# Reordering the attention stretch of a hybrid decoder step: three merged job streams, half-row gathers for every sample query, and prompt heads in pairs

## The chip, the cores and the metric

The program runs on one core of one Trainium2 chip. Its engines are TensorE (PE in the rows, with PEld for its weight loads), VectorE (DVE), ScalarE (ACT), GpSimd (POOL) and SyncE (SP). The metric is the device time of one execution, in microseconds. Runs of one kernel agree within about 0.3% as a rule.

## The reference, cut to what matters

One layer of a decoder is computed for a prompt of 512 tokens and for 64 sample tokens (8 sequences of 8), in f32. The part that this change touches is token mixing:

```python
def select_keys(scores, q_pos, topk):
    masked = jnp.where(key_pos <= q_pos, scores, -jnp.inf)
    _, idx = lax.top_k(masked, topk)

def attend_selected(q, kg, vg, valid):
    logits = jnp.einsum('bqhd,bqkhd->bqhk', q, kg) * (HEAD_DIM ** -0.5)
    p = jax.nn.softmax(jnp.where(valid, logits, -jnp.inf))
    return jnp.einsum('bqhk,bqkhd->bqhd', p, vg)

glu = a_glu * jax.nn.sigmoid(b_glu)
c = jax.nn.silu(layer_norm(causal_depthwise_conv(buf, conv_w, conv_b)))
conv_branch = c @ w_conv_out
attn_branch = o.reshape(B, T, ATT_W) @ w_attn_out
mix = (gc * conv_branch + ga * attn_branch) @ w_o
```

The prompt (8 heads of 64, 512 rows) attends to the 128 best keys of each row, the samples each to the 256 best keys out of 4096 cached ones and their own 8. For the samples the chosen rows of the cache are fetched: one row holds the key and the value of all heads, 2 x 512 f32. A mixture of experts follows, which the change does not touch.

## The kernel before

Every engine runs a list of instructions in a fixed order and waits on semaphores. The order of the stretch in question is computed in Python before the program is built, by a small model of the engines, and written out as two lists: ATTENTION (jobs of TensorE, which ScalarE follows in the same order) and VJOBS (VectorE's). The jobs:

- **Sample**, in 16 groups g of 4 queries. GpSimd issues the gathers (two indirect DMAs of 128 rows for each query). `T g.j` turns the keys of query j (8 transposes, `turn_keys`, L1116), `QK` computes logits (L1128, L1134), `EX` is the exponential on ScalarE, `PT` turns the weights (L1143, L1144), `PV` multiplies by the values (L1152, L1155), `OS` collects the rows (L1162). VectorE adds `max`, `sum` and `om` for each group. A group's gathers may start only when QK (for keys) and PV (for values, or whole rows) of the group before are done, since there is one set of buffers.
- **Prompt**. `pi t.h` gives the indexer's scores of tile t and head h (L1213). VectorE weighs and adds them (`pi`, L1942) and picks 128 keys of a row in 16 `round`s of MAX8 and MATCH_REPLACE8 (L1951, L1952); `bias` makes the mask. Then come 32 units u, 8 heads for each of 4 tiles, with 1 to 4 blocks of 128 keys: `qk u` (L1222), `unit u` on VectorE (L1958 to L1960), an exponential on ScalarE, `weigh u` on VectorE (L1967, L1968), `pt u` (L1229) and `pv u` (L1235). Tile 0 needs no mask from the rounds.
- **Branches**. Gates `gc` and `ga` (L1076, a 128 x 288 job has 16 matmul instructions), the depthwise convolution of channels 256 to 511 in 62 `conv` taps on VectorE (L1925, L1927), its norm `cv`, `croot`, `cn` (with `cstat`, `cnorm`, `csilu` on VectorE), and the products `cb` and `ab` (L1265; VectorE's parts are L2025 and L1988 with L1989).

In TensorE's order before, one prompt stream holds all of prompt and branches; sample jobs are slipped in where the model says that they can start. The gathers of a group are, for the first two queries (`AHEAD = 2`), keys and values apart (`gather_half`, L982), and for the last two whole rows (`gather_rows`, L975), which wait until PV of the group before is done. VectorE does the whole convolution first, then the rounds, and most of the 32 units after them. The expression `hand_over` (L1514) is ScalarE's copy from PSUM to one of four buffers from which VectorE reads.

Ahead of this stretch the sample top-k runs on VectorE; the last thing that TensorE waits for there is `offs` (L1209), the physical rows of the chosen keys. Behind it come `oT`, `abS`, the output projection, the router and the experts.

## Time and profile before

| | before |
|---|---|
| device time, median of 3 | 1457.71 us (1456.45 to 1466.41) |
| span of the profiled execution | 1455.5 us |
| PE busy | 1293.9 us (89%) |
| DVE busy | 711.7 us (49%) |
| ACT busy | 447.8 us (31%) |
| POOL busy | 498.3 us (34%) |

The times of the three executions are device times; the profiled execution has only its span, from the first to the last instruction. The median lies 2.2 us above that span. A busy TensorE is not one at its peak: the granted clock stands beside it in the views by stretch, 1.00 being 2.4 GHz and 0.50 being 1.2 GHz. The stretch that the change reorders reaches from the job `offs` at 370 us to the last `abP` near 879 us.

### The profile page before, as it was taken

The page shows a single profiled execution, that of the slowest core. Times are in us where ns is not written, and L with a number is a line of the kernel's source. Part 1 is how long each engine was busy: PE and PEld are TensorE (multiplying, and loading weights), DVE is VectorE, ACT ScalarE, POOL GpSimd, SP SyncE. Part 2 cuts the span into 40 slices and gives each one's busy share as a digit, 9 for nine tenths or more (in the row PEclk, how much of TensorE's full clock was granted, in tenths as well). Part 3 has the DMA queues.
Part 4 walks back from the last instruction along what each step waited for, and adds up shares of the span by engine and source line. Part 5 has one row for each costly group of instructions (what it writes and reads, how often), then busy time and mean ns, then how long its engine had stood idle before and what let it go on. Part 6 is the DMA issues. An engine that isn't in the chain of part 4 may idle for free.

```text
span 1455.5 us, 19176 instructions
## 1 busy us (share of the span) xinstructions
PE 1293.9 (89%) x7452; PEld 811.2 (56%) x7452; DVE 711.7 (49%) x1362; ACT 447.8 (31%) x932; POOL 498.3 (34%) x455
## 2 busy tenths in 40 slices
PE   5699999896798667998999999998979899999986
PEld 5624777675563333554566647886855454555442
DVE  2409999999998993333410022434432222222215
ACT  1550134353234368544543321222111111111110
POOL 1300086879644412443533310000023343444420
PEclk9899999998898766999999997999889999999998
DMA  7601212122444413555746452028029999999945
GB/s 265 230 13 58 62 58 81 46 79 91 132 150 160 167 55 111 186 186 164 225 129 196 161 207 95 29 95 342 27 86 416 388 416 419 373 406 419 410 169 197
DMA packets 86873, 272.95 MB, mean 188 GB/s; under 512 B 16280, under 2 KB 48744, under 8 KB 75832
## 3 DMA queue, kind: packets, MB, share of 16 engines
q1 hardware_dynamic: 49776, 157.25, 28.2%
q0 software_dynamic: 34528, 111.21, 22.6%
q10 hardware_dynamic: 2479, 3.27, 0.7%
q8 instruction: 60, 0.98, 0.3%
q14 instruction: 30, 0.24, 0.0%
HBM read 292.55 MB, written 22.98 MB: 217 GB/s over the span
## 4 chain that ended last, share of the span: by engine, by line
PE 53%; DVE 26%; DMA 12%; issue 3%; ACT 3%; POOL 2%; ACTq 0%; SPq 0%; POOLq 0%; DVEq 0%
PE ps L1416 9%; PE ps L1076 6%; DVE arena L1852 5%; DVE arena L1851 5%; DVE arena L1853 5%; PE ps L1440 5%; PE ps L1082 5%; PE ps L1265 5%; PE ps L1273 4%; DMA arena<-in_cache_kv,arena 3%; DMA arena<-scr_x,arena 3%; PE ps L1116 3%; PE ps L1134 2%; DMA arena<-in_w_dn,arena 2%; PE ps L1152 2%
## 5 line engine op out<-in xcount | busy, mean ns | idle before, releaser
L1076 PE MATMUL ps<-arena 128*128 128x288 f32 (+4 forms) x1216 | 315.9, 425 | 3.9 <-ACT arena L1642 3.3
L1076 PEld LDWEIGHTS ps<-arena 128*128 128x128 f32 (+1 forms) x1216 | 228.6, 200 | 88.1 <-issue 31.1
L1416 PE MATMUL ps<-arena 128*64 128x256 f32 x1568 | 192.1, 388 | 4.3 <-DMA arena<-in_w_gu 2.0
L982 POOL DMA_INDIRECT arena<-in_cache_kv,arena x128 | 127.1, 993 | 158.5 <-PE ps L1134 121.7
L1416 PEld LDWEIGHTS ps<-arena 128*64 128x64 f32 x1568 | 110.0, 139 | 83.6 <-issue 28.7
L1514 ACT ACTIVATE arena<-ps 128x256 f32<-128x256 f32 (+6 forms) x144 | 59.1, 419 | 217.9 <-PE ps L1265 60.6
L1025 POOL DMA_INDIRECT arena<-scr_x,arena x49 | 49.7, 1014 | 184.9 <-DVE arena L2221 170.3
L1032 POOL DMA_INDIRECT scr_ypair<-arena x49 | 50.4, 1029 | 181.2 <-ACT arena L1784 174.1
L954 POOL TENSOR_TENSOR arena<-arena 128x816 f32<-128x816 f32 x58 | 103.0, 1775 | 17.2 <-ACT arena L1532 10.4
L1440 PE MATMUL ps<-arena 128*64 128x512 f32 x392 | 98.1, 623 | 11.5 <-DMA arena<-in_w_dn,arena 11.5
L1082 PE MATMUL ps<-arena 128*128 128x256 f32 (+4 forms) x544 | 106.4, 359 | 1.8 <-ACT arena L1648 1.2
L975 POOL DMA_INDIRECT arena<-in_cache_kv,arena x64 | 63.6, 994 | 126.0 <-PE ps L1155 109.3
L1116 PE MATMUL ps<-arena 128*128 128x128 f32 x512 | 78.2, 300 | 29.2 <-DMA arena<-in_cache_kv,arena 16.9
L1082 PEld LDWEIGHTS ps<-arena 128*128 128x128 f32 (+1 forms) x544 | 93.2, 195 | 14.5 <-issue 2.7
L1116 PEld LDWEIGHTS ps<-arena 128*128 128x128 f32 x512 | 63.1, 153 | 57.3 <-DMA arena<-in_cache_kv,arena 25.1
L2227 DVE COPY arena<-ps 128x512 f32<-128x512 f32 x49 | 33.9, 692 | 112.5 <-PE ps L1398 112.5
L1548 ACT ACTIVATE arena<-ps 128x512 f32<-128x512 f32 x128 | 70.4, 596 | 60.1 <-PE ps L1116 59.3
L2242 DVE COPY arena<-ps 128x128 f32<-128x128 f32 x49 | 14.3, 292 | 143.1 <-PE ps L1426 143.1
L1265 PE MATMUL ps<-arena 128*128 128x288 f32 (+2 forms) x256 | 78.6, 466 | 0.6 <-ACT arena L1678 0.6
L1851 DVE MAX8 arena<-arena 128x8 f32<-128x2052 f32 x32 | 73.6, 2299 | 1.1
L1852 DVE FIND_INDEX8 arena<-arena 128x8 uint32<-128x2052 f32 x32 | 73.3, 2290 | 0.0
L1853 DVE MATCH_REPLACE8 arena<-arena 128x2052 f32<-128x2052 f32 x32 | 73.0, 2280 | 0.0
(335 smaller groups left out, 1717.5 us busy)
## 6 DMA issues: line engine op xcount, KB each, us to landing
arena<-in_w_gu SPq DMA_DIRECT2D x32, 2048.0 KB, 12.8
arena<-in_w_dn SPq DMA_DIRECT2D x32, 1024.0 KB, 14.8
arena<-in_w_in SPq DMA_DIRECT2D x20, 1024.0 KB, 5.5
arena<-in_w_o SPq DMA_DIRECT2D x4, 1024.0 KB, 5.5
arena<-in_w_pg SPq DMA_DIRECT2D x4, 1024.0 KB, 9.0
arena<-scr_ypair SPq DMA_DIRECT2D x4, 1024.0 KB, 7.9
arena<-in_cache_kv,arena POOLq DMA_INDIRECT x192, 4.5
arena<-in_x_prompt SPq DMA_DIRECT2D x4, 512.0 KB, 8.0
```

What stands on the lines that cost most here:

```text
L954: nc.gpsimd.tensor_tensor(a[:, 0:CLEN], a[:, 0:CLEN], p[:, 0:CLEN], ALU.add).then_inc(conv_add, 1)
L982: pl.indirect_dma_start(unit_rows[:, 2 * j + t, half * H * HD:(half + 1) * H * HD], None, I["cache_kv"].rearrange("n (h d) -> (n h) d", h= ...
L1076: mm = nc.tensor.matmul(out, w[:, k], hT[:, k, a:b], start=(k == 0), stop=(k == KC - 1))
L1082: mm = nc.tensor.matmul(out, hT[:, k, at:at + rows], w[:, k], start=(k == 0), stop=(k == KC - 1))
L1116: mm = nc.tensor.transpose(PS[4 + m % 2][:, c * P:(c + 1) * P], unit_rows[:, 2 * j + t, c * P:(c + 1) * P], ident)
L1265: mm = nc.tensor.matmul(ps[:, 0:n], w[:, c], src[:, c, at:at + n], start=(c == 0), stop=(c == CC - 1))
L1416: mm = nc.tensor.matmul(PS[2 + p % 2][64 * half:64 * half + 64, 0:2 * P], xT[:, p % 3, j, 64 * h:64 * h + 64], w[:, k, half, :], start=(k ...
L1440: mm = nc.tensor.matmul(PS[5 + p % 2][64 * half:64 * half + 64, :], hidT[:, p % 2, c * 64:c * 64 + 64], w[:, c, half * 512:(half + 1) * 51 ...
L1548: nc.scalar.activation(kts[:, j, :, t * P:(t + 1) * P], PS[4 + m % 2].rearrange("p (c k) -> p c k", c=CC), cp).then_inc(k_act, 1)
L1851: step(V.max(m, work))
L1852: V.max_index(idxu[:, r * 8:r * 8 + 8], m, work)
L1853: step(V.match_replace(work, m, work, TAKEN))
```

## The change

Three streams (sample, prompt, branch) replace two; at each step the stream is taken whose next job could start first by the model, with a random lead for each stream, and of 240 such plans the one is kept in which VectorE's part ends first. The model's costs are new. The indexer jobs now come first, the convolution behind and between them, and prompt units come two at a time: two `qk`, one `pv` for two heads, two `pt`. The `pv` job writes both heads, to the two halves of the PSUM partitions, its matmuls alternating between them. All four sample queries have keys and values gathered apart, keys as soon as QK of the group before is done. The jobs themselves compute the same.

```diff
-AHEAD = 2
@@ prompt_jobs
-    for u in range(UNITS + 3):
-        jobs += [("qk", u)] if u < UNITS else []
-        jobs += [("pt", u - 2)] if 2 <= u < UNITS + 2 else []
-        jobs += [("pv", u - 3)] if u >= 3 else []
-        if norm:
-            jobs += norm.pop(0)
-        elif conv:
-            jobs += [conv.pop(0)]
...
+    jobs = [("ncS",), ("ncP",)] + [("pi", t, h) for t in range(1, PT) for h in range(H)]
+    for u in range(0, UNITS + 4, 2):
+        jobs += [("qk", u), ("qk", u + 1)] if u < UNITS else []
+        jobs += [("pv", u - 4)] if u >= 4 else []
+        jobs += [("pt", u - 2), ("pt", u - 1)] if 2 <= u < UNITS + 2 else []
+    return jobs
+def branch_jobs():
+    jobs = [job for gate in GATES[3:] for job in gate] + [("cv", 0), ("croot", 0)]
     for t in range(NT):
+        jobs += ([("cv", t + 1)] if t + 1 < NT else []) + [("cn", t)] + ([("croot", t + 1)] if t + 1 < NT else [])
+    jobs += [(kind, g, c) for g in range(4) for c in range(2) for kind in ("cbP", "cbS")]
+    jobs += [(kind, g, c) for g in range(4) for c in range(2) for kind in ("gaP", "gaS")]
@@ sample_jobs
-    jobs = [("T", 0, 0), ("T", 0, 1)]
+    jobs = [("T", 0, j) for j in range(GQ)]
     for g in range(NGR):
-        turned = [[("T", g + 1, j)] if g + 1 < NGR else [] for j in range(AHEAD)]
-        jobs += [("T", g, j) for j in range(AHEAD, GQ)] + [("QK", g), ("EX", g), ("PT", g)] + turned[0] + [("PV", g)] + turned[1] + [("OS", g)]
+        turned = [("T", g + 1, j) for j in range(GQ)] if g + 1 < NGR else []
+        jobs += [("QK", g), ("EX", g), ("PT", g)] + turned[:2] + [("PV", g)] + turned[2:] + [("OS", g)]
@@ the merge
-    while prompt or sample:
-        tied = bool(jobs) and jobs[-1][0] == "qk" and jobs[-1][1] >= 2
-        if not sample or (tied and prompt):
-            put(prompt.pop(0))
-        elif not prompt:
-            put(sample.pop(0))
-        else:
-            put((sample if start(sample[0]) <= start(prompt[0]) + 0.3 else prompt).pop(0))
+    while any(streams.values()):
+        half = bool(jobs) and jobs[-1][0] == "qk" and jobs[-1][1] % 2 == 0
+        pick = "prompt" if half else min((k for k in streams if streams[k]), key=lambda k: start(streams[k][0]) + lead[k] + rng.uniform(0, 1))
+        put(streams[pick].pop(0))
+def interleaved():
+    best = None
+    for seed in range(240):
+        rng = np.random.RandomState(seed)
+        lead = {k: rng.uniform(-1, 1) for k in ("sample", "prompt", "branch")}
+        plan = merged(lead, rng)
+        best = plan if best is None or plan[0] < best[0] else best
+    return best[1:]
@@ GpSimd
                 if g:
                     pl.wait_ge(lg_full, g)
-                for j in range(AHEAD):
+                for j in range(GQ):
                     gather_half(g, j, 0, k_in)
                 if g:
                     pl.wait_ge(pv_done, g)
-                for j in range(AHEAD, GQ):
-                    gather_rows(g, j)
-                for j in range(AHEAD):
+                for j in range(GQ):
                     gather_half(g, j, 1, v_in)
@@ TensorE, pv
-                    pe.wait_ge(drained, after("pt", a[0]))
+                    pe.wait_ge(drained, after("pt", a[0] + 1))
                     for j in range(t + 1):
-                        mm = nc.tensor.matmul(ps[o:o + 64, 0:P], vtok[:, j, h * 64:h * 64 + 64], ptile[:, a[0] % 2, j, :],
-                                              start=(j == 0), stop=(j == t))
+                        for i in range(2):
+                            mm = nc.tensor.matmul(ps[64 * i:64 * i + 64, 0:P], vtok[:, j, (h + i) * 64:(h + i) * 64 + 64], ptile[:, i, j, :],
+                                                  start=(j == 0), stop=(j == t))
@@ ScalarE
-                    ins = nc.scalar.activation(oT[o:o + 64, h // 2, t * P:(t + 1) * P], ps[o:o + 64, 0:P], cp)
+                    ins = nc.scalar.activation(oT[:, h // 2, t * P:(t + 1) * P], ps[:, 0:P], cp)
```

TensorE's order at units of tile 2 (three blocks of keys), before. L1222 is `qk`, L1229 `pt`, L1235 `pv`; the rest are sample jobs and `cb` (L1265):

```order
L1222 MATMUL ps<-arena 128x384
L1229 MATMUL ps<-arena 128x128 x2
L1128 MATMUL ps<-arena 8x320 x4
L1134 MATMUL ps<-arena 8x320 x16
L1235 MATMUL ps<-arena 64x128 x2
L1265 MATMUL ps<-arena 128x288 x4
L1222 MATMUL ps<-arena 128x384
L1229 MATMUL ps<-arena 128x128 x2
```

The same place in the new order, where L1216 is `qk`, L1223 `pt` and L1229 `pv` of two heads, L1110 the key transposes and L1146 with L1149 the sample values:

```order
L1216 MATMUL ps<-arena 128x384 x2
L1229 MATMUL ps<-arena 64x128 x4
L1110 MATMUL ps<-arena 128x128 x8
L1146 MATMUL ps<-arena 8x512 x8
L1149 MATMUL ps<-arena 8x512 x4
L1223 MATMUL ps<-arena 128x128 x2
L1110 MATMUL ps<-arena 128x128 x16
L1223 MATMUL ps<-arena 128x128 x2
L1216 MATMUL ps<-arena 128x384 x2
```

Two `qk` now stand together, with two `pt` between them and the next two, and all four key transposes of a group lie around its values. The `cb` jobs left this place; they stand behind the units.

VectorE's order at units of tile 1, before (L1958 to L1960 `unit`, L1967 and L1968 `weigh`, L2039, L2045 sample work, L2015 to L2020 the convolution's norm):

```order
L1958 TENSOR_TENSOR arena<-arena 128x256
L1959 TENSOR_REDUCE arena<-arena 128x1
L1960 TENSOR_SCALAR arena<-arena 128x1
L1967 RECIPROCAL arena<-arena 128x1
L1968 TENSOR_SCALAR arena<-arena 128x256
L2039 RECIPROCAL arena<-arena 128x1
L2015 RECIPROCAL arena<-arena 64x1
L2016 TENSOR_SCALAR arena<-arena 64x512
L1958 TENSOR_TENSOR arena<-arena 128x256
```

The same units in the new order; L1942 and L1943 are MAX8 and MATCH_REPLACE8 of a round for tile 2, L1949 to L1951 `unit`, L1958 and L1959 `weigh`:

```order
L1943 MATCH_REPLACE arena<-arena 128x384
L1942 MAX arena<-arena 128x8
L1943 MATCH_REPLACE arena<-arena 128x384
L1949 TENSOR_TENSOR arena<-arena 128x256
L1950 TENSOR_REDUCE arena<-arena 128x1
L1951 TENSOR_SCALAR arena<-arena 128x1
L1958 RECIPROCAL arena<-arena 128x1
L1959 TENSOR_SCALAR arena<-arena 128x256
```

Before, all 48 rounds stand ahead of unit 5; now 16 stand ahead of unit 8 and 32 between units 9 and 24, always between two pairs. GpSimd's order where the gathers begin, before (the first rows are the last of the convolution's products, L975 a gather of whole rows, L982 one of half rows):

```order
L922 TENSOR_TENSOR arena<-arena 128x512
L924 COPY arena<-arena 128x8x8
L982 DMA arena<-in_cache_kv,arena 128x512 x4
L975 DMA arena<-in_cache_kv,arena 128x1024 x4
L982 DMA arena<-in_cache_kv,arena 128x512 x8
L975 DMA arena<-in_cache_kv,arena 128x1024 x4
```

and so on, 12 gathers for a group: 4 halves of keys, 4 whole rows, 4 halves of values. The same place in the new order (L978 is the gather of half rows, L995 and L1019 already belong to the experts):

```order
L925 TENSOR_TENSOR arena<-arena 128x512
L927 COPY arena<-arena 128x8x8
L978 DMA arena<-in_cache_kv,arena 128x512 x256
L995 MEMSET arena 128x3072
L1019 DMA arena<-scr_x1,arena 128x512 x6
```

The whole rows are gone, and a group has 16 gathers: 8 of keys and behind them 8 of values.

## Rows read from the trace of the kernel before

**Rows 1.** Head of the page: the span, and busy time of each engine.

```profile
span 1455.5 us, 19176 instructions
PE 1293.9 (89%) x7452; PEld 811.2 (56%) x7452; DVE 711.7 (49%) x1362; ACT 447.8 (31%) x932; POOL 498.3 (34%) x455
```

**Rows 2.** Five stretches: length, busy PE, PEld, DVE, ACT, POOL, granted clock, DMA, GB/s.

```profile
370.00:450.00 80.00, 71.50 (x406) 47.89 (x406) 74.03 (x159) 27.18 (x53) 39.59 (x36) 0.95 0.53 173
450.00:525.00 75.00, 50.88 (x318) 25.33 (x317) 69.57 (x186) 36.93 (x74) 26.95 (x29) 0.80 0.42 135
525.00:600.00 75.00, 54.91 (x291) 28.42 (x292) 36.57 (x108) 53.55 (x122) 20.05 (x21) 0.68 0.30 99
600.00:740.00 140.00, 133.74 (x872) 75.13 (x874) 52.16 (x143) 69.42 (x175) 62.63 (x63) 0.99 0.58 184
740.00:880.00 140.00, 136.92 (x746) 81.61 (x738) 18.23 (x36) 43.47 (x75) 41.52 (x44) 1.00 0.52 172
```

**Rows 3.** Waits of PE, 370 to 866 us: us in total, times, longest.

```profile
PE ps L1116 <- DMA arena<-in_cache_kv,arena: 16.9, 13, 3.4
PE ps L1229 <- DVE arena L1968: 10.0, 3, 6.2
```

**Rows 4.** Timeline of PE: start, length, instruction, and the idle time before it.

```profile
370.38 0.44 PE L1209 MATMUL ps<-arena 64*128 64x64 f32 x2 [18.38 <-DVE arena L1882]
...
559.68 3.80 PE L1134 MATMUL ps<-arena 128*8 128x320 f32 x32
...
868.04 10.57 PE L1265 MATMUL ps<-arena 128*128 128x512 f32 x24
```

**Rows 5.** Timeline of DVE: the first convolution tap, and the reduce of group 4.

```profile
379.30 0.92 DVE L1925 TENSOR_SCALAR arena<-arena 128x512 f32<-128x512 f32 x2
...
527.19 0.49 DVE L2033 TENSOR_REDUCE arena<-ps 128x1 f32<-128x320 f32 x1
```

**Rows 6.** DVE groups by shape, 370 to 866 us: busy us, mean ns, idle before.

```profile
L2025 DVE TENSOR_TENSOR arena<-arena 128x288 f32<-128x288 f32 x16 | 7.3, 459 | 30.2 <-ACT arena L1514 30.2
L1958 DVE TENSOR_TENSOR arena<-arena 128x512 f32<-128x512 f32 x8 | 5.5, 693 | 14.6 <-ACT arena L1514 14.6
L1959 DVE TENSOR_REDUCE arena<-arena 128x1 f32<-128x512 f32 x8 | 5.5, 686 | 0.3
L1968 DVE TENSOR_SCALAR arena<-arena 128x512 f32<-128x512 f32 x8 | 4.0, 495 | 0.3
L1988 DVE TENSOR_TENSOR arena<-arena 128x512 f32<-128x512 f32 x4 | 2.8, 694 | 19.6 <-ACT arena L1514 19.6
```

**Rows 7.** Timeline of PE where it runs without a stop: heads of tile 3.

```profile
701.02 1.12 PE L1222 MATMUL ps<-arena 64*128 64x512 f32 x2
...
706.26 2.21 PE L1265 MATMUL ps<-arena 128*128 128x288 f32 x8
...
709.45 0.66 PE L1229 MATMUL ps<-arena 128*128 128x128 f32 x4
...
719.69 1.09 PE L1235 MATMUL ps<-arena 128*64 128x128 f32 x8
```

**Rows 8.** Timeline of PE: one sample group beside five gate jobs, and an `ab` job.

```profile
792.14 4.15 PE L1076 MATMUL ps<-arena 128*128 128x288 f32 x16
...
806.14 8.03 PE L1076 MATMUL ps<-arena 128*128 128x288 f32 x32
...
823.12 4.15 PE L1076 MATMUL ps<-arena 128*128 128x288 f32 x16
...
857.08 3.60 PE L1265 MATMUL ps<-arena 128*128 128x512 f32 x8
```

**Rows 9.** Timeline of POOL: two gathers of half rows in a row.

```profile
417.08 0.95 POOL L982 DMA_INDIRECT arena<-in_cache_kv,arena  x1 [0.30 <-issue]
418.34 1.38 POOL L982 DMA_INDIRECT arena<-in_cache_kv,arena  x1 [0.30 <-issue]
```

**Rows 10.** The instructions of line 982: time from a gather's issue to landing.

```profile
DMA to landing us min/median/max: 3.2/4.0/7.9
```

More of the change, by code:

```diff
@@ L226, in vector, with pending, gather @@
         dve_end[job] = dve
-        if waiting and waiting[0][0] != "conv":
-            background(dve + vector_time(waiting[0]) + 0.01)
     def settle(last):
-        nonlocal dve
         while any(last(job) for job in waiting):
-            vector_order.append(waiting.pop(0))
-            dve += vector_time(vector_order[-1])
-    def gather(g, first, free):
+            aside()
+    def pending(last):
+        return sum(vector_time(j) for j in waiting[:max([n + 1 for n, j in enumerate(waiting) if last(j)], default=0)])
+    def gather(g, keys, free):
         nonlocal pool
         pool = max(pool, free + 0.3)
-        for j in range(first, first + 2):
+        for j in range(GQ):
             pool += 2.5
-            landed[("T", g, j)] = pool + (2.3 if first < AHEAD else 4.7)
-        if first >= AHEAD:
-            pool += 5.0
-            landed[("PV", g)] = pool + 2.8
+            landed[("T", g, j) if keys else ("PV", g)] = pool + (2.3 if keys else 2.8)
     def start(job):
@@ L260, in start @@
             t = max(t, dve_end[("om", a[0])])
-        elif kind == "pi" and a == (1, 0):
-            t = max(t, dve + sum(vector_time(j) for j in waiting) - 4)
+        elif kind == "qk":
+            wait = pending(lambda j: j[0] == "bias" and j[1] <= a[0] // H)
+            t = max(t, dve + wait - 1.0) if wait else t
         elif kind == "pt":
@@ L272, in start @@
             t = max(t, dve_end[("csilu", NT - 1)])
+        elif job == ("gaP", 0, 0):
+            t = max(t, pe_end.get(("qk", UNITS - 1), 1e9))
+        elif job == ("abP", 0, 0):
+            t = max(t, act_end[("pv", UNITS - 2)])
         return t
@@ L993, in _ @@
                     pl.wait_ge(pv_done, g)
-                for j in range(AHEAD, GQ):
-                    gather_rows(g, j)
-                for j in range(AHEAD):
+                for j in range(GQ):
                     gather_half(g, j, 1, v_in)
```

86 lines of the change are left out of this document (33 added, 53 removed).

## The prediction

> **What bounds the kernel now.** The head of the page [rows 1] has TensorE busy for 89% of 1455.5 us, and nothing else over half. That is an average. I read the stretch that the change reorders in five pieces [rows 2]. From 370 to 525 us VectorE is busy for 74.0 of 80 and 69.6 of 75 us, so it sets the pace, while TensorE is only filling in (50.9 of 75, at a clock of 0.80). From 525 to 600 no engine is full: TensorE 54.9 of 75 at 0.68, VectorE 36.6, ScalarE 53.6. Here chains from engine to engine decide (head scores, mask, exponential, weights, turn, with the convolution's norm between them). From 600 to 880 TensorE is busy for 270.7 of 280 us at 0.99 and 1.00: it is the bound. The waits agree: TensorE's idle time in the stretch is in small pieces behind gathers (16.9 us) and behind VectorE's `weigh` (10.0 us) [rows 3].
>
> The stretch begins when TensorE gets the row numbers, at 370.38, and ends with `abP` at 868.04 + 10.57 = 878.6 [rows 4]: 508 us. Everything ahead of it keeps its order, and everything behind starts when it ends. So the question is when the last `abP` ends.
>
> **How I cost an order.** With fixed lists, the end can't come before VectorE's work up to a point plus TensorE's work behind the job that waits for this point. In the new order the largest such sum is at `weigh 23`, for which `pt 23` waits: all rounds, the whole convolution and 25 of 32 units stand ahead of it on VectorE.
>
> VectorE's share: it was busy for 250.6 us from 370 to 880 [rows 2], of which at most 9 lie before 379.30, where it leaves the lists for the convolution [rows 5], and one `abP` of 1.4 comes later: 243 us. Where it never waits it shows 69.57 busy of 75 (93%), the rest being small gaps between dependent instructions; 243 / 0.93 = 261 us of pace. Behind `weigh 23` stand 7 units of 0.693 + 0.686 + about 0.15 = 10.8; 8 `weigh` of 0.495 + about 0.16 = 5.2; 16 `cb` of 0.459 = 7.3; 8 `abP` of twice 0.694 = 11.1 [rows 6]; and 8 sample groups. The last piece of rows 2 prices these: 18.23 less seven `abP` (9.7) leaves 8.5 for four to five groups, 2 each, 16 in all. Sum 50.4, with gaps 53. So 208 us are ahead, and VectorE passes the point at 379.3 + 208 = **587**.
>
> TensorE's share behind it: 8 sample groups, 16 `ga`, 16 `cb`, 8 `abP`, 6 `qk`, 9 `pt`, 5 pairs in `pv`. From 792.14 to 823.12 TensorE did one group and five gate jobs without a real stop [rows 8]; two gate jobs are 8.03, so five are 20.1 and a group is 10.9. Then: groups 87 (two turns are already done, one `OS` is more: 86), `ga` 64, `cb` 16 x 2.14 = 34, `abP` 8 x 3.53 = 28, `qk` 6 x 1.06 = 6, `pt` 9 x 0.6 = 5, `pv` 5 x 1.0 = 5 [rows 7, 8], each a row's length less 0.07 of overlap. Sum **229**.
>
> The bound is 587 + 229 = **816**, against 878.6 now. How good is such a sum? The same way, the old order gives VectorE's `max 4` after 151 us of pace, at 530; the trace has it at 527.19 [rows 5]. The part in which VectorE is full is thus priced within 3 us. The old order's own largest sum is at `max 5`: 379.3 + 175 + 293 = 847, and it needed 878.6, **31 us more**, nearly all in 525 to 600, where TensorE's 54.9 busy us at 0.68 are only some 37 of full-speed work. That excess is what I have to guess anew.
>
> **Part by part.**
>
> *Rounds and convolution between the units.* No work goes away. In 525 to 600 VectorE had nothing left to fill with: its rounds were over before unit 5, and eight heads and most of the norm jobs ran bare. In the new order 32 rounds lie between the pairs of units 9 to 24, some 5 us for each of eight pairs, about what one trip TensorE, ScalarE, VectorE takes. What is late next is VectorE itself, until 587. Excess there: between 0 (as from 370 to 525) and 31 (as now); I take 11, nearer the full stretch, which it resembles, with pairs that have few rounds (20 to 23 have none between them) counted bare.
>
> *The indexer jobs first.* VectorE starts with `pi 1.0`, which waits for ScalarE, and that engine first issues nine output DMAs for `ncP`. VectorE would be free at 379.3; I take 2 us, bounds 0 and 5.
>
> *Gates moved.* `gc` jobs stand between the groups 0 to 3; `cb` and `ga` after the units. They fill TensorE's time only. They cost nothing while VectorE is behind, and they are in the 229 where it isn't.
>
> *Gathers.* 64 more, each 0.95 us of GpSimd plus 0.30 to the next [rows 9]: 80 us more on GpSimd, and 20 us a group instead of 15. Keys no longer wait for PV: the last two queries' rows, which cause most of the 16.9 us in [rows 3], are asked for right after QK. The last key half is issued 0.4 + 7 x 1.25 = 9.2 us after QK and lands 4.0 later [rows 10], at 13; TensorE has 6 to 8 us of the group's own jobs and 8 to 15 of other jobs by then. From QK 9 to QK 14 stand five groups (55), 15 `cb` (32), 5 gate jobs (20) and the last heads' four `pt` and three `pv` (5): 112 us, 22 a group, just over GpSimd's 20. I take 9 us of stops for the eight groups behind the point, bounds 2 and 24.
>
> The trace shows both prices of a half-row gather: 0.95, and 1.38 in the time when VectorE ran its two-input convolution taps [rows 9]. The Trainium skill ("SBUF — State Buffer", section "SBUF: two separate sides") says that VectorE and GpSimd share one port pair under an exclusive lock, and that descriptors can't be written while VectorE holds it. By that rule alone every gather beside a busy VectorE would be stretched; the row beside it at 0.95, in the same taps, says not each one.
>
> *Pairs in `pv`.* 32 jobs become 16. For four blocks one head takes 1.09 us [rows 7], 8 matmuls of 128 columns. If two heads share the time, 10 to 11 us of TensorE's work go, of which only the five pairs behind the point count (5 us, in the sum as half). If not, 5 us come back. The nearest row is the QK of [rows 4]: 32 instructions over 320 columns, written to four strips, in 3.80 us. One `qk` of [rows 7] needs 0.53 us an instruction for 512 columns, 0.33 for 320, so one after the other they would need 10.6. They run in parallel, so I take the sharing.
>
> The Trainium skill says against it ("TensorE: Matmul & The Clock Gate", section "Part 3: Packing small matmuls — row/col tiling") that a weight load overlaps matmuls in flight only if the row group differs, and both heads here use all rows. By it the pair would take as long as two heads, and the sum would be 5 us more. No row of before has this shape, so it stays open.
>
> *Smaller things.* One ScalarE activation and one VectorE copy ahead of the queries go, some 0.6 us, and 16 of ScalarE's copies of `pv`; ScalarE isn't full anywhere.
>
> **Sum.** 816 + 2 + 11 + 9 = 838, so 40 us earlier than 878.6, less 1 because TensorE leaves VectorE's pace with a low clock: 39. Span 1455.5 - 39 = 1416.5. The median of the three runs lies 2.2 above the profiled span: **1419 us**.
>
> **Rivals.**
>
> 1. *Lock step of the heads* (the other side). On TensorE, `pt` of a pair waits for `weigh`, and behind it stand the next `qk`, and the PV, QK and turns of a sample group. If the rounds between do not cover the trip, VectorE waits for the next `qk` and both stand. From 525 to 600 the eight heads cost 75 - 37 = 38 us, 4.7 a head. The new order has 24 heads (8 to 31) in this pattern; at 4.7 it would lose 113 and end at 929, 50 us later: 1508. With 3.5 a head it is 900, or 1479; with 2.6 a head no time changes. So it decides from 2.6 a head. For it: ScalarE was close behind TensorE in that piece (53.6 of 75), and it keeps nearly all of that work. Against: the norm jobs that filled it are now spread over groups 3 to 8, and the rounds cover eight of twelve pairs.
>
> 2. *GpSimd becomes the bound.* If each gather takes 1.38 + 0.30, a group takes 27 us; groups 10 to 14, with 112 us of TensorE's work, would take 135. That is 23 more, with 9 already counted: 1419 + 14 = 1433; were groups 4 to 9 slowed as well, 1445. Against: from 740 on VectorE is nearly idle, and only its taps went with long issues. The lock rule of the Trainium skill named above would bring this out.
>
> 3. *The order fits better than I think.* Excess 5 instead of 22: 1402.
>
> 4. *Nothing gained.* TensorE's total work hardly shrinks, so if its order had already been full, nothing would change. The 30% of idle or slow clock from 450 to 600 speaks against it. A mixture of 1 and 2 ends here all the same, at 1450 to 1460.
>
> **Chances.** Forecast with its own range of 1408 to 1432: 0.60. Rival 3: 0.12. Rival 2: 0.12. Rival 4: 0.09. Rival 1: 0.07. About 1% (14.6 us) is what a measurement here can tell from no change. Faster by over 1% (below 1443): 0.60 + 0.12 + 0.11 = 0.83; within 1%: 0.10; slower: 0.07. The range from **1400 to 1444** leaves out rivals 1 and 4 and a little on either end.
>
> **What would show it.** Right: VectorE over 90% busy from 381 to about 590, the `max` of group 8 near 605, TensorE at 1.00 from there on with groups of 21 to 25 us, the last `abP` near 839, TensorE's wait for gathers below 10 us. The point `weigh 23` not before 587 and not after 610. Wrong: VectorE at 75% or less between units 8 and 24, with waits for ScalarE's `hand_over` copies over 30 us (rival 1); GpSimd without waits for QK and PV in groups 10 to 14, and TensorE waiting for gathers there (rival 2); 16 matmuls of a `pv` pair in 2 us instead of 1 (the pairs don't share). Any change of more than 3 us ahead of 370 or behind the last `abP` would also be outside of what I see.

## The result, and the profile after

The changed kernel takes **1444.0 us** (median of 4 runs, 1442.7 to 1445.9) beside 1458.7 for the kernel before (with a fourth run of it): ratio 0.989, 95% interval 0.987 to 0.992. Forecast were 1419 us, with a range of 1400 to 1444: the direction is right, the size is not, 14.6 us instead of 39. The head of the page, which answers to [rows 1]:

```profile
span 1441.6 us, 19201 instructions
PE 1272.4 (88%) x7452; PEld 802.8 (56%) x7452; DVE 709.7 (49%) x1361; ACT 439.4 (30%) x912; POOL 563.2 (39%) x519
```

The same five stretches as [rows 2], with the same columns:

```profile
370.00:450.00 80.00, 71.72 (x445) 43.08 (x446) 66.91 (x159) 41.50 (x98) 48.98 (x46) 0.89 0.52 151
450.00:525.00 75.00, 56.21 (x346) 34.90 (x348) 65.90 (x181) 38.84 (x82) 44.60 (x44) 0.83 0.58 172
525.00:600.00 75.00, 55.23 (x417) 29.05 (x409) 61.31 (x163) 51.47 (x119) 41.28 (x43) 0.84 0.50 145
600.00:740.00 140.00, 123.17 (x811) 72.80 (x812) 38.91 (x99) 55.67 (x121) 82.95 (x85) 0.89 0.61 186
740.00:880.00 140.00, 134.20 (x685) 85.08 (x684) 20.66 (x46) 36.87 (x68) 37.81 (x40) 0.95 0.45 146
```

VectorE works 61.3 us from 525 to 600 where it had 36.6: rounds now fill between the heads, as meant. But it is at 82% and not over 90%, and TensorE has 20 us of holes there, at a clock of 0.84. From 600 to 740 TensorE had 6 us of holes before; now it has 17, at a clock of 0.89. TensorE's waits from 370 to 866 (us in total, times, longest) answer to [rows 3]:

```profile
PE ps L1110 <- DMA arena<-in_cache_kv,arena: 30.6, 14, 4.3
PE ps L1203 <- DVE arena L1874: 18.7, 1, 18.7
PE ps L1110 <- ACT arena L1542: 15.3, 16, 5.7
PE ps L1137 <- ACT arena L1548: 8.3, 6, 2.3
PE ps L1223 <- DVE arena L1959: 4.5, 2, 2.4
```

The 18.7 lie ahead of `offs`. The turns (L1110) wait 30.6 us for gathers, 16.9 before, and 15.3 for ScalarE's copies (L1542). VectorE's `weigh` went from 10.0 to 4.5. The two points on which the sum stood, `weigh 23` and the `max` of group 8, on VectorE's timeline, and on TensorE's the last `abP`:

```profile
614.40 0.42 DVE L1959 TENSOR_SCALAR arena<-arena 128x384 f32<-128x384 f32 x1
...
627.63 0.48 DVE L2024 TENSOR_REDUCE arena<-ps 128x1 f32<-128x320 f32 x1
```

```profile
849.64 12.61 PE L1259 MATMUL ps<-arena 128*128 128x512 f32 x29
```

`weigh 23` is passed at 614.4 (forecast 600), the last `abP` ends at 849.64 + 12.61 = 862.25, that is 862.3 (forecast 839; before 878.6, [rows 4]). Below, this end is "the end of the stretch".

**Stop 1, the gathers.** GpSimd issues the values of one group, then the keys of the next. Its rows, and TensorE's in the same time (the first is the end of one PV, the last the end of the next):

```profile
745.32 0.94 POOL L978 DMA_INDIRECT arena<-in_cache_kv,arena  x1 [5.35 <-PE ps L1149]
...
754.07 0.95 POOL L978 DMA_INDIRECT arena<-in_cache_kv,arena  x1 [0.30 <-issue]
755.32 0.95 POOL L978 DMA_INDIRECT arena<-in_cache_kv,arena  x1 [0.30 <-issue]
```

```profile
743.98 1.04 PE L1149 MATMUL ps<-arena 64*8 64x512 f32 x8
...
760.13 1.09 PE L1110 MATMUL ps<-arena 128*128 128x128 f32 x8 [0.53 <-DMA arena<-in_cache_kv,arena]
...
764.94 1.04 PE L1110 MATMUL ps<-arena 128*128 128x128 f32 x8
...
767.74 1.04 PE L1149 MATMUL ps<-arena 64*8 64x512 f32 x8
```

Values go out when PV has ended (745.0), eight of them until 755.0, and only then the keys, though the QK for which they wait ended at 751.3. The first sample's second gather starts at 756.57 and has landed when T starts at 760.13, 3.6 us later. The new order puts two turns **ahead** of PV. So PV waits for turns, these for keys, these for the values queued ahead of them, and these for the PV before: a loop, here of 23.8 us. I had counted GpSimd's 20 us a group and no loop. In this place TensorE has gate jobs to run meanwhile and stands only 0.5 us for the gather; where it has less, it stands longer. One such place lies right ahead of `weigh 23`: a turn that stands ahead of PV of group 7 on TensorE, and VectorE's `om` of that group (L2036), which stands ahead of `weigh 23` in VectorE's order:

```profile
601.28 1.97 PE L1110 MATMUL ps<-arena 128*128 128x128 f32 x8 [4.30 <-DMA arena<-in_cache_kv,arena]
```

```profile
610.59 0.75 DVE L2036 SCALAR_TENSOR_TENSOR arena<-ps,arena 128x512 f32<-128x512 f32 x1 [5.86 <-PE ps L1149]
```

VectorE has its rounds behind it, stands 5.9 us for that PV, and passes `weigh 23` 3.9 us after the PV's end.

**Stop 2, ScalarE.** ScalarE's rows where a tile of the convolution's norm passes (start, length), and TensorE waiting for it:

```profile
547.87 1.28 ACT L1692 ACT_TABLE_LOAD   x1
549.17 0.46 ACT L1692 ACTIVATE arena<-ps,arena 128x128 f32<-128x128 f32 x1
...
552.12 1.28 ACT L1532 ACT_TABLE_LOAD   x1
...
555.01 1.28 ACT L1497 ACT_TABLE_LOAD   x1
...
556.57 1.08 ACT L1542 ACTIVATE arena<-ps 128x512 f32<-128x512 f32 x2
```

```profile
557.30 3.87 PE L1110 MATMUL ps<-arena 128*128 128x128 f32 x16 [4.02 <-ACT arena L1542]
...
573.57 1.12 PE L1110 MATMUL ps<-arena 128*128 128x128 f32 x4 [3.34 <-DMA arena<-in_cache_kv,arena]
576.70 2.92 PE L1110 MATMUL ps<-arena 128*128 128x128 f32 x12 [2.02 <-ACT arena L1556]
```

From 547.4 to 556.5 ScalarE does eight activations for the norm and two heads' exponentials, and changes its table three times: sigmoid, exponential, square root. The copy of the keys stands behind all of it. From 450 to 600 there are 17 table loads, 15 of them for these three functions:

```profile
L1497 ACT ACT_TABLE_LOAD x5 | 6.4, 1283 | 0.1
L1692 ACT ACT_TABLE_LOAD x5 | 6.4, 1283 | 0.0
L1532 ACT ACT_TABLE_LOAD x5 | 6.4, 1283 | 0.1
```

In these rows a change costs 1.28 us and nothing after it: the load at 552.12 is followed by an activation at 553.42. The Trainium skill ("ScalarE: Activation LUTs", section "What ACT_TABLE_LOAD costs") has the same 1283 ns, but with a drain of about 1380 ns on top; this trace shows none, and the measurement decides.

### The profile page after: what moved, and what is told of

Its sections match the earlier page's. It is cut to its first block, busy times and chain, and to the rows that moved or that the text cites. A ratio compares the mean times of both kernels' runs of the same rounds, so it can differ in the third digit from the quotient of the medians.

```text
span 1441.6 us, 19201 instructions
## 1 busy us (share of the span) xinstructions
PE 1272.4 (88%) x7452; PEld 802.8 (56%) x7452; DVE 709.7 (49%) x1361; ACT 439.4 (30%) x912; POOL 563.2 (39%) x519
## 3 DMA queue, kind: packets, MB, share of 16 engines
q0 software_dynamic: 35552, 111.22, 24.1%
## 4 chain that ended last, share of the span: by engine, by line
PE 52%; DVE 23%; DMA 12%; POOL 5%; ACT 4%; issue 4%; ACTq 0%; SPq 0%; POOLq 0%; DVEq 0%
PE ps L1410 9%; PE ps L1070 6%; DVE arena L1844 5%; DVE arena L1843 5%; DVE arena L1845 5%; PE ps L1434 5%; PE ps L1076 5%; POOL arena L978 4%; PE ps L1259 4%; PE ps L1267 4%; PE ps L1110 3%; DMA arena<-scr_x,arena 3%; DMA arena<-in_cache_kv,arena 3%; PE ps L1146 2%; DMA arena<-in_w_dn,arena 2%
## 5 line engine op out<-in xcount | busy, mean ns | idle before, releaser
L978 POOL DMA_INDIRECT arena<-in_cache_kv,arena x256 | 255.6, 998 | 181.0 <-PE ps L1149 81.5
L1070 PE MATMUL ps<-arena 128*128 128x288 f32 (+4 forms) x1216 | 312.7, 423 | 3.9 <-ACT arena L1636 3.3
L1110 PE MATMUL ps<-arena 128*128 128x128 f32 x512 | 83.0, 313 | 48.4 <-DMA arena<-in_cache_kv,arena 30.6
L1019 POOL DMA_INDIRECT arena<-scr_x,arena x49 | 49.7, 1014 | 185.3 <-DVE arena L2212 170.7
L1110 PEld LDWEIGHTS ps<-arena 128*128 128x128 f32 x512 | 66.0, 160 | 72.5 <-DMA arena<-in_cache_kv,arena 36.4
L1542 ACT ACTIVATE arena<-ps 128x512 f32<-128x512 f32 x128 | 71.0, 596 | 61.9 <-PE ps L1110 61.6
L1770 ACT ACTIVATE arena<-ps 128x128 f32<-128x128 f32 x49 | 13.6, 278 | 180.7 <-PE ps L1410 180.7
## 6 DMA issues: line engine op xcount, KB each, us to landing
arena<-in_w_dn SPq DMA_DIRECT2D x32, 1024.0 KB, 15.6
```

The lines of the kernel that those rows point to most:

```text
L978: pl.indirect_dma_start(unit_rows[:, 2 * j + t, half * H * HD:(half + 1) * H * HD], None, I["cache_kv"].rearrange("n (h d) -> (n h) d", h= ...
L1070: mm = nc.tensor.matmul(out, w[:, k], hT[:, k, a:b], start=(k == 0), stop=(k == KC - 1))
L1110: mm = nc.tensor.transpose(PS[4 + m % 2][:, c * P:(c + 1) * P], unit_rows[:, 2 * j + t, c * P:(c + 1) * P], ident)
L1542: nc.scalar.activation(kts[:, j, :, t * P:(t + 1) * P], PS[4 + m % 2].rearrange("p (c k) -> p c k", c=CC), cp).then_inc(k_act, 1)
```

## The experiments

Each line of the table is one kernel. "Time" is the median of its executions, the ratio is to the kernel before on the same chip, "profiled" is the time of the one execution whose trace was kept, and "end" is the end of the stretch in that trace. Executions of one kernel lie up to 12 us apart (e12: 1420.5 to 1432.3, or 0.8%, where 0.3% is given as the rule above), so an end is only as good as its execution: that of e6 is the fastest of four, 5 us below the median.

| kernel | time, us | ratio, 95% | profiled, us | end, us |
|---|---|---|---|---|
| changed | 1444.0 | 0.989 (0.987-0.992) | 1443.4 | 862.3 |
| e1, both turns behind PV | 1433.3 | 0.982 (0.979-0.985) | 1432.5 | 854.8 |
| e11, one turn behind PV | 1430.0 | 0.979 (0.975-0.982) | 1432.0 | 849.5 |
| e14, no table loads | 1421.0 | 0.973 (0.968-0.977) | 1420.5 | 847.1 |
| e6, fewer rounds | 1442.6 | 0.989 (0.985-0.993) | 1437.6 | 857.7 |
| e8 = e1 + e14 | 1424.6 | 0.975 (0.971-0.978) | 1427.9 | 851.1 |
| e9b = e1 + e6 | 1430.0 | 0.980 (0.975-0.984) | 1428.0 | 848.2 |
| e15 = e14 + e6 | 1425.2 | 0.974 (0.969-0.978) | 1425.7 | 849.4 |
| e9 = all three | 1409.6 | 0.966 (0.962-0.970) | 1408.3 | 833.7 |

Where table loads are out, the router gets other numbers, and less is fetched later: 266.7 MB in all instead of 273.0. What follows the end then takes 572 to 575 us instead of 576 to 581, so there a time says more than the stretch gave, and I go by both.

**The loop, opened.** Both turns moved, in the finished order:

```
+for _g in range(NGR - 1):
+    for _j in (1, 0):
+        ATTENTION.remove(("T", _g + 1, _j))
+        ATTENTION.insert(ATTENTION.index(("PV", _g)) + 1, ("T", _g + 1, _j))
```

> The changed kernel, its order kept but for one thing: the two turns T(g+1,0) and T(g+1,1), which stand ahead of PV(g) on TensorE, now stand right behind it. Theory A (a loop through the gathers): in the changed kernel GpSimd issues the value gathers of group g behind PV(g-1) (8 x 1.25 = 10.1 us), then the key gathers of group g+1 (about 5 us until the first two samples' rows are asked for, 3.7 us until they land), and only then can TensorE turn them and run PV(g) (2.8 us or more): 24 us at least from one PV to the next, 27.0 in the mean of the profile. With the turns behind PV the loop falls to GpSimd's own 16 gathers, 20.6 us. A expects PV to PV at 24 to 25 us in the mean, TensorE's waits for gathers at less than 15 us instead of 30.6, and a time of 1424 to 1434. Theory B (the heads' chains between TensorE, ScalarE and VectorE set the pace, gathers only fill the slack): PV comes earlier but the last abP does not, time 1440 to 1446. Theory C (TensorE's own work and its clock set the time): 1442 to 1450, since two turns less stand between the exponential and PV, where they hid it.

Time and gather waits came as theory A says, 1433.3 us and 6.7 us. TensorE's waits:

```profile
PE ps L1114 <- ACT arena L1546: 22.1, 35, 4.5
...
PE ps L1114 <- DMA arena<-in_cache_kv,arena: 6.7, 6, 2.4
```

But the period did not, which A put at 24 to 25 us: from the first PV to the last are 401.8 us, 26.8 a group, against 27.0. The first PV comes 4.5 us earlier (412.5 instead of 417.0), the ninth 11.5, the last 7.5. And the stops moved: the turns, now four in a row, wait 22.1 us for ScalarE. With one turn alone moved (`for _j in (1,)`):

> The changed kernel with only T(g+1,1) moved behind PV(g); T(g+1,0) stays ahead of it. Loop theory: the loop through the gathers falls by two gathers, 2.5 us, from 24 to 21.5, just under TensorE's work per group; the one turn ahead of PV still covers the copy of the weights. Gather waits of TensorE 8 to 16 us instead of 30.6, time 1431 to 1437, near the 1433.3 of both turns behind. If only TensorE's four turns in a row made the difference: 1438 to 1444.

The time is 1430.0 us, 1 below the expected range and the same as e1's within the intervals. The waits are 18.9 us for gathers, over the 8 to 16 expected, and 14.4 for copies. Here the first PV comes 0.9 us later and the last 12.8 earlier, 26.1 us a group: this run, more than e1, shows that the loop lengthens the period.

**Fewer gathers.** `for t in range(2 if half == 0 or g == 0 else 1)` in the gather of values.

> The changed kernel with the value gathers of one key block in two left out from the second group on: the second 128 values of a sample are those of the first group (the result is not the reference's). GpSimd issues 12 gathers a group instead of 16, 5 us less; nothing else changes. Theory A (the loop PV, value gathers, key gathers, turns, PV at 24 us): the loop falls to about 19 us and TensorE's work per group, 22 us in the mean, becomes the bound; gather waits of TensorE below 10 us instead of 30.6; time 1422 to 1432. Theory B (heads' chains): 1440 to 1445. Rival D (it is GpSimd's sum, 20 us a group, and not the loop): gather waits fall by less than 10 us, time 1436 to 1441.

1438.7 us (0.986, 0.982 to 0.989), gather waits 19.6. A's time is missed and rival D's is met, though the gather waits fell by 11.0 us and not by less than 10: 5 us a group less on GpSimd are worth 5 in all. So the loop isn't the whole story.

**The two parts of the change by themselves.** The kernel before with `AHEAD = 4` behind the line that fixes its order, so that all gathers are half rows:

> The kernel before, its order of jobs kept word for word, with the gather part of the change alone: keys and values of all four samples of a group as half rows, 16 gathers a group instead of 12. Only one of the next group's turns stands ahead of PV there. Before, 16.9 us of TensorE's time went to waits for gathers. If the gathers bring what they were priced at in the prediction's step, these waits fall below 6 us and the time is 1445 to 1452. Theory B (in 525 to 660 the heads' chains decide, and gathers are covered there): 1452 to 1458. If more gathers hurt by themselves (contention with VectorE, GpSimd's 20 us a group instead of 15): 1460 to 1470.

1452.5 us (0.995, 0.993 to 0.998), gather waits 5.9 of 16.9: the gathers alone bring some 7 us. That lies between the first theory, whose wait it meets, and B, whose time it meets. And the changed order with the old gathers:

> The changed kernel with its order kept, and the gathers of the kernel before put back: samples 2 and 3 as whole rows behind PV. All theories agree on the direction and not on the size: T(g+1,2) and T(g+1,3) stand right behind PV(g), and their rows are asked for only when PV(g) has ended, 0.4 + 4 gathers of about 1.25 + 5 us landing, 9 to 10 us. If nothing else slows, TensorE stands 6 to 9 us in each of 15 groups for gathers, less what the loop through the turns gives back (GpSimd has four gathers a group less, 5 us): 50 to 110 us, 1490 to 1550. If it comes out below 1460, the order alone carries the gain and the gathers none of it.

1569.8 us (1.074, 1.070 to 1.078), beyond my bound of 1550. TensorE's waits for gathers from 370 to 900 us:

```profile
PE ps L1122 <- DMA arena<-in_cache_kv,arena: 120.7, 36, 7.8
```

The order needs the gathers. A third kernel has the gathers in the kernel before, with its order worked out anew:

> The kernel before with the gather part of the change alone: keys of all four samples and then values of all four as half-row gathers, the first two turns of the next group ahead of PV, the other two behind; the merge of two streams stays, with its costs, and its order is worked out again with the new landing times. Theory A: the same loop of 24 us stands in this kernel, but its groups were 30.2 us apart before, so the loop does not bind; the 16.9 us of gather waits fall to below 8. Time 1448 to 1456 (before: 1458.7). Theory B says the same of this kernel. If the gathers themselves were the harm (a sum of 20 us a group against 15, contention with VectorE), this kernel would be slower than before: 1462 to 1475.

1498.0 us (1.025, 1.022 to 1.029). It says nothing on the price of gathers, since its order puts the heads late (`weigh 23` at 799). But there the samples run almost bare, and the loop is seen pure; the ends of three PVs and the turn between two of them:

```profile
640.87 1.04 PE L1152 MATMUL ps<-arena 64*8 64x512 f32 x8
...
657.18 1.97 PE L1113 MATMUL ps<-arena 128*128 128x128 f32 x8 [6.37 <-DMA arena<-in_cache_kv,arena]
...
665.00 1.04 PE L1152 MATMUL ps<-arena 64*8 64x512 f32 x8
...
689.89 1.04 PE L1152 MATMUL ps<-arena 64*8 64x512 f32 x8
```

24.1 and 24.9 us a round. The eight transposes behind the stop of 6.4 us take 1.97 us instead of 1.09: the granted clock is 0.50 there, so this stop costs more than its length.

**VectorE's length.** Two lines in `select_round`: `if t > 1 and r % 2: return`.

> The changed kernel with every second top-k round of the tiles of 384 and 512 columns left out (8 of 32 rounds' worth of VectorE work, some 22 us, most of it ahead of weigh 23; the result is not the reference's). The prediction's step: VectorE is full until weigh 23, and the rest of TensorE's work comes behind it. By that step the end comes 15 to 22 us earlier: 1422 to 1429, and weigh 23 is passed at 593 to 600 instead of 614. Theory A (the gather loop sets the time of the groups from the third on, VectorE waits inside it): PV ends hardly move, weigh 23 by less than 8 us, time 1436 to 1442. Theory B (head chains): rounds were what filled VectorE's waits, so weigh 23 moves by less than 5 and the time is 1439 to 1444.

1442.6 us, in B's range and 0.6 above A's. `weigh 23` comes at 612.2, 2.2 us earlier, for 22 us less of work. The prediction's step, VectorE full until `weigh 23`, is refuted as the cause. VectorE gives part of the time gained on the rounds away again, standing 9.3 us instead of 5.9 for the PV of group 7:

```profile
608.40 0.75 DVE L2038 SCALAR_TENSOR_TENSOR arena<-ps,arena 128x512 f32<-128x512 f32 x1 [9.26 <-PE ps L1149]
```

**ScalarE's tables.** In the norm's activations, `ACT.Sigmoid` becomes `ACT.Identity`, and `ACT.Sqrt` becomes a copy. First on top of e1, then, since that fitted, on the changed kernel itself:

> The kernel with the turns behind PV (1433.3), with ScalarE's sigmoid and square root of the convolution's norm replaced by functions that need no other table (the result is not the reference's): about 15 table loads of 1.28 us go from 450 to 600 us, some 19 us of ScalarE's time, nothing else. Theory B (from 507 to 609 us the pace is that of the chains TensorE, ScalarE, VectorE, TensorE, with ScalarE's blocks of the norm jobs between the copies that TensorE's turns wait for): weigh 23 is passed 6 to 12 us earlier than 609, time 1421 to 1428. If VectorE or TensorE's work sets the pace there, weigh 23 moves by less than 3 us, and the time is 1431 to 1435.

> The changed kernel, its order kept with the loop through the gathers, and ScalarE's sigmoid and square root of the norm replaced by functions that need no other table (the result is not the reference's). Without the loop this gave 8.7 us. Theory L (limits in layers): the gather loop holds PV to PV at 24 us, so of the 8.7 only part shows, 2 to 6 us: 1438 to 1442. If the limits simply add (each stop costs its own length, wherever it is): 1434 to 1437.

The first came in B's range of time, 1424.6, though `weigh 23` came 4.2 us earlier, at 605.1, and not 6 to 12. The second did not come as expected: 1421.0 us instead of 1438 to 1442, so my picture of the loop as an outer limit is wrong. `weigh 23` comes at 602.4 instead of 614.4 and the end 15.2 us earlier, with the loop and 33 us of gather waits in place. From 507 to 600 (changed, then e14):

```profile
507.00:600.00 93.00, 63.07 (x454) 34.35 (x452) 75.61 (x206) 63.45 (x148) 50.40 (x53) 0.79 0.51 149
```

```profile
507.00:600.00 93.00, 68.94 (x500) 36.46 (x498) 79.38 (x213) 51.55 (x143) 55.96 (x59) 0.83 0.58 168
```

12 us less on ScalarE, 6 us more done on TensorE. TensorE's turns wait 8.2 us for copies instead of 15.3, so the copies are only part of the gain; which of ScalarE's other followers brings the rest, no run separates. From the PV of group 5 to that of group 6, where the rows of stop 2 are, the changed kernel takes 32.8 us and e14 26.6.

**All together.**

> The kernel with the turns behind PV (1433.3), table loads in place, and every second top-k round of the tiles of 384 and 512 columns left out (the result is not the reference's). Theory L: with the gather loop gone, but ScalarE's blocks still there, VectorE's cut of 22 us brings part: weigh 23 comes 3 to 8 us before 609, time 1426 to 1431. Theory N: less than 2 us, 1431 to 1434.

> The kernel with the turns behind PV and without ScalarE's table loads in the norm (1424.6), and every second top-k round of the tiles of 384 and 512 columns left out as well (the result is not the reference's). In the changed kernel this cut of 22 us on VectorE moved weigh 23 by 2.2 us and the time by 1.4. Theory L (limits in layers: the gather loop and ScalarE's blocks hid VectorE's length; with both gone ScalarE stands up to 7.3 us for a unit that VectorE has behind its rounds, and the copies of TensorE's turns stand behind that): weigh 23 now comes 6 to 12 us before 605, the time is 1413 to 1419. Theory N (VectorE's length never matters here): weigh 23 moves by less than 3 us, 1422 to 1426.

> The changed kernel with its gather loop, without the table loads of the norm and with every second top-k round of the tiles of 384 and 512 columns left out (the result is not the reference's). Without the loop the same two cuts gave 23.7 us, to 1409.6. Theory L: the loop of 24 us a group holds from unit 8 to unit 24, some five groups, so 8 to 14 us of it show: 1430 to 1436. If the loop hid nothing of the rounds: 1420 to 1424.

1430.0 us is in L's range; 1409.6 is below L's (1413 to 1419), and 1425.2 is not in L's range but 1 above the other. By the medians the 22 us of VectorE bring 1.4 us in the changed kernel, 3.3 without the loop, nothing without the loads (4.2 later), and **15.1** without both; by the ends 4.6, 6.6, 2.3 later and 17.4. Only the last is clear of the scatter. With the loop in place VectorE stands for the PV of group 7 instead (9.8 us in e15). What stands behind VectorE once the loop is gone is seen in e8, on ScalarE and on TensorE:

```profile
575.18 0.61 ACT L1536 ACTIVATE arena<-arena 128x384 f32<-128x384 f32 x1 [7.30 <-DVE arena L1955]
```

```profile
577.06 3.87 PE L1114 MATMUL ps<-arena 128*128 128x128 f32 x16 [4.73 <-ACT arena L1546]
```

ScalarE stands 7.3 us for a unit's maximum, which VectorE computes behind its rounds, and the copies of the turns stand behind it on ScalarE. So VectorE does reach TensorE, through ScalarE's queue, once nothing else is later. From 507 to 600 e9 has the clock at 0.93:

```profile
507.00:600.00 93.00, 75.88 (x598) 38.43 (x600) 65.98 (x184) 59.11 (x163) 61.43 (x64) 0.93 0.64 183
```

**Without leaving work out.** On ScalarE the exponential of a pair's first head goes behind the turns' copies that follow it:

```
+                if late and kind not in ("T", "pv", "croot", "PV", "OS", "QK"):
+                    exponentials(late.pop())
...
+                if kind == "qk" and a[0] % 2:
+                    late.append(a[0] - 1)
```

> The kernel with the turns behind PV (1433.3); on ScalarE the exponential of the first head of a pair is issued behind the copies of the turns that follow it, where such copies follow, instead of right behind the second head's copy. No work is added or left out. Theory L: TensorE's waits for the copies of its turns (22.1 us in 35) come from ScalarE standing for VectorE's unit with the copies behind it; they fall by 5 to 10 us, and the time is 1425 to 1431, less what weigh loses by the later exponential. Rival M: weigh stands as long for the exponential as the copies gain, and pt with it: 1431 to 1438.

> The changed kernel with T(g+1,1) alone moved behind PV(g), and ScalarE's exponential of a pair's first head issued behind the copies of the turns that follow; nothing is left out. Alone, the first gave 14.0 us against the changed kernel, and the second 3.8 against the kernel with both turns behind PV. If they add: 1425 to 1428. If the second only repaired the four turns in a row, which this order does not have: 1429 to 1432.

On e1: 1429.4 us (0.979, 0.976 to 0.982), in L's range. But the waits for copies, which L has falling by 5 to 10 us, go only from 22.1 to 21.9 (the longest from 4.5 to 2.5), and the intervals of e1 and e10 overlap: neither L's mechanism nor a gain is shown. With one turn moved: **1428.4** (0.976, 0.971 to 0.981), the fastest full kernel here, though its interval overlaps those of e10 and e11. I can't say that the two add.

**The pairs.** The loops over `i` and `j` exchanged, so that one head follows the other:

> The changed kernel with the two heads of a pv pair one after the other: all matmuls of head h, then all of h+1, instead of alternating between the two halves of the columns. The prediction took 10 to 11 us of TensorE's work in all for the sharing, 5 of it behind weigh 23. The profile has the pair of four blocks at 1.09 us for 16 matmuls, as one head took before. If alternation is what lets them share, four-block pairs rise to 2.0 us, the five pairs behind weigh 23 and the tightly followed ones before it bring 4 to 8 us: 1448 to 1452. If they share in this order too, 1443 to 1446.

A pair of four blocks, in the changed kernel and with the heads apart:

```profile
628.67 1.09 PE L1229 MATMUL ps<-arena 128*64 128x128 f32 x16
```

```profile
627.17 1.58 PE L1229 MATMUL ps<-arena 128*64 128x128 f32 x16
```

Alternating, two heads take what one took [rows 7]; one after the other, 1.58, not the 2.0 expected. The next job begins 1.03 and 1.51 us after these starts, so the difference is not only one of modelled ends. The time is 1440.3 (0.987, 0.983 to 0.991), no different from the changed kernel's within the intervals. The prediction took from the Trainium skill ("TensorE: Matmul & The Clock Gate", section "Part 3: Packing small matmuls — row/col tiling") that a pair would take two heads' time. That was read too narrowly: the section has weight loads overlapping only between different row groups, but it also measures three tiles side by side in the columns at 2.38 times the speed. The rows agree that column tiles share time; that the order of the matmuls decides how much, only the rows show.

**Left open by a disturbed set.** Three more kernels have to be read beside a kernel before that itself took 1470.4 us, instead of 1459 to 1461 beside the others.

> The changed kernel with T(g+1,1) alone behind PV(g), and without the norm's table loads (sigmoid and square root replaced, the result is not the reference's). If the loop's stops and the loads cost separately, the 14.0 of the one turn come off the 1421.0 of the loads: 1407 to 1412. If they are the same time counted twice (what stands for ScalarE would else have stood for the gathers), the last abP stays near the 847 of the loads alone and the time is 1417 to 1423. The mean of the two, 1412 to 1417, says partly.

> A full kernel: one turn moved behind PV, the deferred exponential (1428.4), and the norm's sigmoid as 1 / (1 + exp(-y)): ScalarE writes y with four copies and then one exponential over the tile, VectorE adds one, takes the reciprocal and multiplies. It saves ScalarE the sigmoid's table load five times, most of the reloads behind them and three activations a tile, some 15 us, and adds VectorE two instructions of 512 columns a tile, by its rows 0.55 us for the one, the other unknown, 5 to 10 us in all. If ScalarE's blocks are what the time hangs on: 1418 to 1424. If VectorE's new work takes the place: 1426 to 1432.

e16 took 1450.3 us (0.986, 0.982 to 0.989), with fewer rounds as well (e17) 1450.5 (0.985, 0.981 to 0.989) where 8 to 15 us below e16, or within 3 us of it, were expected, and e18 1463.9 (0.996, 0.993 to 0.999). In e16 ScalarE was idle for some 158 us in waits for nothing that the profile shows, 3.7 in the changed kernel; the two largest such lines:

```profile
ACT arena L1773 <- issue: 71.9, 22, 3.3
ACT arena L1551 <- issue: 24.6, 4, 6.6
```

All three have them (158, 170 and 132 us), and VectorE's grew too (72.5 us in e16, 23.5 in the changed kernel). So these times judge neither theory. Whether one turn and no loads add, and whether the exponential form of the sigmoid gains, stays open.

## Why the prediction was right and wrong

- **The frame held.** The end of the stretch moved by 16.3 us, the span by 13.9; ahead of it nothing moved, behind it 2.5 us came back.
- **TensorE's work behind `weigh 23`: right.** Forecast 229; busy 232.2 from 614.4 to 862.2 at a clock of 0.96, and 227.5 at 0.99 in e1.
- **"Excess there: I take 11": the step that failed.** The sum took VectorE to be full until `weigh 23`, at 587, put 2 us for the indexer jobs and 11 for everything else on top, and had rounds between the pairs cover the trips from engine to engine. Measured: `weigh 23` at 614.4, so 25 us in place of the 11. VectorE's work was priced right: it was busy 192 us from 379.3 to 614.4, forecast 193. But it was busy 83% of the time from 381 to 590, not over 90%, and its work was not what `weigh 23` hung on: 22 us less moved the point by 2.2. The last to come was the PV of group 7, and what held TensorE before it, from 504 to 614, were waits of its turns: 12.5 us for gathers and 12.1 for ScalarE's copies. Without the table loads the point comes at 602.4, with the loads in and one turn behind PV at 607.3, with both turns behind it at 609.3. I wrote "ScalarE isn't full anywhere" and went by its busy share; 15 table loads, 19.2 us, and the norm's activations stand as blocks ahead of the copies. The loads are tested by a run; the activations beside them are not.
- **"9 us of stops for gathers": right where it was put, and put in too few places.** Behind `weigh 23` TensorE waits 9.0 us for gathers, as forecast. It stands 15.6 in all there and is busy 3.2 more than forecast, with the clock at 0.96: 247.8 us instead of 238. But 21.6 of the stretch's 30.6 us of gather waits lie ahead of `weigh 23`, where the sum has no term for them. The step took GpSimd's sum of 20 us and missed that two turns ahead of PV chain keys behind values; its hint was in the order's rows, where T(g+1) stands before PV(g).
- **The keys "right after QK": wrong.** In 15 groups GpSimd waited only 7 times for QK (24.3 us); in the other 8 the keys queued behind the values.
- **Pairs and the gather's price: right.** A pair takes 1.09 us; a gather takes 0.95 in the median and 1.00 in the mean of 256. Rival 2's 1.38 as a rule did not come, nor its sign: from 640 to 780 GpSimd stands 32 us for PV and QK. Its result, TensorE waiting for gathers, came by another way. The sentence that by the lock every gather beside a busy VectorE would be stretched was drawn too wide: up to 600 us, where VectorE is busy over 80%, 26 of 131 gathers took over 1.1 us and 98 took less than 1.0.
- **Rival 1** is right in kind, chains from engine to engine, not in place or size: between units 8 and 24 VectorE is busy 77%, near its sign of 75%, but it waits only 4.3 us for `hand_over` copies, not over 30.

The 24 us missing at the end of the stretch are thus 14.4 ahead of `weigh 23` and 9.8 behind it. By cause they are no simple sum. Taking out one thing moves the end by 4.6 us (rounds), 7.5 (both turns; 12.8 for one turn) or 15.2 (loads), and all three at once by 28.6. By the medians the same cuts bring 1.4, 10.7 (14.0), 23.0 and 34.5 us, of which the loads' share falls in part behind the end. Loads with turns move the end by 11.2 and loads with rounds by 12.9, less than the loads alone, but the times (1424.6, 1425.2 and 1421.0) have overlapping intervals, so this is not shown to be more than scatter; the waits for copies (25.8 us in e8, 8.2 in e14) would be a reason. What is clear of it is that the rounds bring nothing beside the loop and some 15 us with loop and loads gone. Of differences below 5 us between single ends I make nothing, and the kernels ran on several chips, on which the kernel before took 1458.7 to 1461.3.

## What to carry to other kernels

- A pacing sum over one engine's work finds the bound only if no other in-order queue feeds it or stands between it and the waiter: read what is queued ahead of the instruction waited for, on each engine that it passes, not the busy share of its engine.
- When requests of two kinds share a queue and each is released by a different step, follow the circle (step, request, landing, consumer, step) and price it as well as the queue's sum.
- A part that brings nothing when removed alone may be covered: try it again with the cover gone before calling it free. Look also at what grew in its place (here the stand for PV, from 5.9 to 9.3 us).
- An end read from one trace scatters as its execution does. Put the median beside it before explaining a few microseconds.

## What the runs showed of the hardware

- Two `pv` heads on the two column halves (128 rows x 64 columns of f32 weights each, 128 columns moving) run 16 matmul instructions in 1.09 us if they alternate, in 1.58 if not, at full clock in both.
- TensorE's clock can fall in a short stop. Behind a stop of 4.3 us in the changed kernel the granted clock was 0.50, and eight transposes took 1.97 us instead of 1.09; behind one of 4.0 in e1 the first 16 matmuls of PV took 3.60 instead of 1.90. Behind a stop of 2.8 us at 693 in the changed kernel eight transposes took 1.10, so not every stop did this.
- An activation table's change costs 1.28 us, and the activation behind it starts within 0.02 us.
- A gather of 128 half rows costs GpSimd 0.95 us and 0.30 to the next, and lands 3.7 us after its issue in the median.
